# Fewer, longer f32 stretches between the projection's matmuls in a hybrid decoder layer

## What is computed

```python
u = rmsnorm(h, norm_w)
proj = jnp.einsum('btd,dc->btc', u, w_in)
...
dec_strict = jnp.exp(jnp.where(strict, diff, -jnp.inf))
A = beta[..., None] * jnp.einsum('bhtd,bhsd->bhts', k, k) * dec_strict
lhs = jnp.eye(C, dtype=A.dtype) + A
rhs = jnp.concatenate([beta[..., None] * v, (beta * jnp.exp(gam))[..., None] * k], axis=-1)
sol = lax.linalg.triangular_solve(lhs, rhs, left_side=True, lower=True)
```

## Time and profile before

| quantity | value |
|---|---|
| median of 3 runs | 692.07 us (691.67 to 693.25) |
| time of the profiled execution | 692.72 us, of which span 690.9 us |
| PE, matmuls | 673.3 us busy (97%), 4,585 instructions |
| PE, weight loads | 640.8 us busy |
| DVE | 413.5 us busy (60%) |
| ACT | 324.2 us busy (47%) |
| POOL | 375.8 us busy (54%) |
| mean granted TensorE clock | 0.995 of full speed |

### The profile page before, as it was taken

The page is one execution under the profiler, slowest core; times in us unless marked ns, Lnnn a source line. Parts: engine busy times, 40 slices in busy tenths (PEclk is TensorE's granted clock), DMA queues, the critical chain, the costliest instruction groups (busy, mean ns, idle before and its releaser), DMA issues. The chain is left out here.

```text
span 690.9 us, 13130 instructions
## 1 busy us (share of the span) xinstructions
PE 673.3 (97%) x4585; PEld 640.8 (93%) x4585; DVE 413.5 (60%) x977; ACT 324.2 (47%) x918; POOL 375.8 (54%) x581
## 2 busy tenths in 40 slices
PE   6999999999999999999999999999999999999995
PEld 4799999989999999999999999999999998888884
DVE  7836446278882472597933634888426257866256
ACT  7545432746654416466445254555452354242333
POOL 4547342268773343587824343887442559866324
PEclk9999999999999999999999999999999999999998
DMA  8744334221214347532548332023254325212014
GB/s 277 72 45 83 31 35 84 27 32 32 42 34 62 51 74 37 24 24 37 39 57 72 70 43 31 2 39 51 55 85 145 90 64 189 85 55 84 1 61 183
DMA packets 64004, 44.96 MB, mean 65 GB/s; under 512 B 17446, under 2 KB 59044, under 8 KB 63940
## 3 DMA queue, kind: packets, MB, share of 16 engines
q1 hardware_dynamic: 63764, 43.81, 36.0%
q10 hardware_dynamic: 176, 0.33, 0.1%
HBM read 35.88 MB, written 7.65 MB: 63 GB/s over the span
## 5 line engine op out<-in xcount | busy, mean ns | idle before, releaser
L283 PE MATMUL proj<-uTh,w_high 128*128 128x352 f32 (+4 forms) x768 | 262.0, 341 | 0.0
L283 PE MATMUL proj<-uTh,w_low 128*128 128x352 f32 (+4 forms) x768 | 245.7, 320 | 0.0
L283 PE MATMUL proj<-uTl,w_high 128*128 128x352 f32 (+4 forms) x768 | 245.2, 319 | 0.0
L283 PEld LDWEIGHTS proj<-uTh,w_high 128*128 128x128 f32 x768 | 145.1, 189 | 0.2
L283 PEld LDWEIGHTS proj<-uTl,w_high 128*128 128x128 f32 x768 | 145.1, 189 | 0.0
L283 PEld LDWEIGHTS proj<-uTh,w_low 128*128 128x128 f32 x768 | 144.3, 188 | 0.0
L326 POOL TENSOR_TENSOR w_low<-w_raw,w_high 128x256 fp32r<-128x256 f32 (+1 forms) x54 | 76.1, 1420 | 47.2 <-DVE decay L379 26.8
L1356 POOL TENSOR_TENSOR level_k<-hg_k,f_suffix 128x64 f32<-128x64 f32 (+1 forms) x144 | 64.4, 467 | 10.5 <-PE mix L1827 5.0
L1366 POOL TENSOR_TENSOR f_suffix<-f_suffix,f_prefix 128x192 f32<-128x192 f32 x84 | 52.3, 622 | 17.8 <-DVE f_prefix L1621 6.0
L1668 DVE SCALAR_TENSOR_TENSOR conv_out<-conv_in,hg_taps,conv_out 128x352 f32<-128x352 f32 (+2 forms) x81 | 55.2, 681 | 0.0
L1621 DVE TENSOR_TENSOR f_prefix<-f_prefix 128x192 f32<-128x192 f32 x84 | 43.9, 523 | 13.9 <-POOL f_suffix L1366 13.1
(11 more groups left out here) (331 smaller groups left out, 1416.3 us busy)
## 6 DMA issues: line engine op xcount, KB each, us to landing
w_raw<-in_w_in SPq DMA_DIRECT2D x32, 512.0 KB, 8.5
x_tile<-in_x SPq DMA_DIRECT2D x8, 512.0 KB, 8.5
w_raw<-y_scratch SPq DMA_DIRECT2D x8, 384.0 KB, 4.4
decay<-gamma_scratch SPq DMA_DIRECT2D x4, 576.0 KB, 3.7
landing<-in_w_out SPq DMA_DIRECT2D x4, 512.0 KB, 7.8
landing<-in_x SPq DMA_DIRECT2D x3, 512.0 KB, 8.3
out_y<-landing SPq DMA_DIRECT2D x3, 512.0 KB, 2.6
y_scratch<-gd_y SPq DMA_DIRECT2D x6, 192.0 KB, 2.6
```

The costliest lines, as they stand in the source:

```text
L283: last = pe.matmul(acc[:, 0:tw], w[j % 2][:, k, :], u[:, k, t0:t0 + tw], start=(k == 0 and i == 0), stop=(k == KT - 1 and i == 2))
```

## The change

The number of projection parts behind the f32 blocks is dealt out anew. Among the groups, three blocks get none behind them, so that A1 of group 0 runs into A1 of 1, A3 of 0 into A1 of 2, and A3 of 1 into A2 of 2: nine stretches of f32 work become six, with the same 32 parts between them. The parts over the small inverses go from 38 to 42. In the levels, parts stand only behind Z4 and Z5 (5 each, `("mixed", i)`): Y4 runs into Z4, TN4 into Y5 and Z5, TN5 into Y6 and Z6, so eight stretches become three. The end of the phase gets 9 parts in place of 4. The order of the f32 blocks, every matmul and every piece stay the same.

On ACT, the three decay exponentials, which stood one in each level, move ahead to the time of the small inverses, before the second half of the parts there. A one-element Silu behind them (`primer`) has ACT load the Silu table at once.

```diff
+        primer = sb("silu_primer", [P, 1], F32, st)
...
-            give((s, g), (4, 4, 4, 4, 4, 3, 3, 3, 3)[n])
+            give((s, g), (0, 7, 5, 0, 7, 5, 0, 5, 3)[n])
         give(("blocks", 0), 10)
-        give(("blocks", 1), 28)
+        give(("blocks", 1), 16)
+        give(("blocks", 2), 16)
         for i in MIXED:
...
-            give(("B1", i), 3)
-            give(("B2", i), 2)
             if i < LEVELS - 1:
-                give(("B3", i), 2)
+                give(("mixed", i), 5)
...
             take_hg(act, parts[("blocks", 1)])
+            if more:
+                for g in range(NG):
+                    decay_exp(act, g, dec_sub, dec_exp)
+                act.activation(primer[:, :], cc[:, 0, 0:1], ACT.Silu)
+            take_hg(act, parts[("blocks", 2)])
...
                 if more:
-                    decay_exp(act, i - BASE, dec_sub, dec_exp)
                     if i == BASE:
                         split_high(act, 4)
...
-                take_hg(act, parts[("B1", i)])
-                take_hg(act, parts[("B2", i)])
                 if i < LEVELS - 1:
+                    take_hg(act, parts[("mixed", i)])
...
-                project(pe, parts[("B1", i)])
...
-                project(pe, parts[("B2", i)])
                 if i < LEVELS - 1:
+                    project(pe, parts[("mixed", i)])
...
-                    project(pe, parts[("B3", i)])
             project(pe, parts[("end",)])
```

More of the change, by code:

```diff
@@ L2124, in _ @@
                         wo_highs(act, (4,))
-                    take_hg(act, parts[("B3", i)])
             take_hg(act, parts[("end",)])
@@ L2297, in _ @@
             project(pe, parts[("blocks", 1)])
+            project(pe, parts[("blocks", 2)])
             for i in MIXED:
```

## The result

The changed kernel takes 694.58 us (median of five runs, 694.19 to 695.05); the kernel before takes 691.86 us beside it (five runs, 691.47 to 693.25). The ratio is 1.0036, with a 95% interval of 1.0024 to 1.0047: slower by 0.4%, some 2.5 us. (The ratios in this document are worked out from the single runs of both kernels; they are not the quotients of the medians.) The forecast was 694.0 us.

A forecast was written before the change was run, and what follows sets the result against it. PE alone was taken to bound the delta phases. Waits for ACT's copies, 0.41 to 0.56 us a phase, taken as 1.9 us over four phases, added to the 692.07 us median gave 694.0 us; range 691.2 to 696.5 us.

The forecast's parts named there:

- Joining saves nothing: Joined blocks among the groups and joined Y and Z: 0.00 us saved each, bounds 0 and 0.08.
- Rival 2: Each change between projection and f32 work costs 0.08 us: 689.4 us without waits (12%), 691.3 us with them (5%).
- Level 4 to 5: Behind TN4, Y5's first matmul waits for ACT's copy of group 0: 0.15 us lost a phase.
- the allowance: Up to 0.05 us extra at each of three waiting places, for one more step in PE's queue; an estimate.
- Level 5 to 6: Behind TN5, Y6 waits for ACT's copy, shorter transposes hiding less: 0.23 us lost a phase.
- Y to Z: Z waits for ACT's copy of Y, tightest at group 2 of level 6: 0 to 0.03 us lost.
- The sum: Waits in the levels: 0.41 us a phase, 0.56 with allowances; four phases 1.6 to 2.2 us, taken as 1.9.
- The groups: Group blocks keep their places to within one part and nothing new is awaited there; no cost counted.
- The moved exponentials: ACT's chain ahead of the second hg_v copy is hidden before the fourth weight tile: price 0, cover 1.5 us.
- rival 3: ACT's chain ends over 1.5 us later than forecast, PE waits at the fourth weight tile: 697.3 us, chance 7%.
- The fewer table loads are worth nothing.: Two ACT table loads a phase in place of four gain nothing, since ACT's time was not on PE's path.
- The drain behind a table load: The skill's extra 1.38 us per table switch does not show; by that rule PE loses some 1.2 us in three phases.

The follow-up runs named there:

- the exponentials alone: Kernel before with only the three decay exponentials and the one-element Silu moved ahead, f32 blocks where they were: 692.49 us against 692.20, ratio 1.0004.
- more hand-overs: Kernel before with 60 more changes between projection and f32 work, same matmuls: 693.21 us against 692.82, ratio 0.9998.
- the groups alone: Kernel before with only the parts among the group blocks dealt out anew: 692.87 us against 692.82, ratio 1.0003.
- one part behind each TN, old groups: Changed kernel with one of five parts put behind TN4 and TN5, and the groups' parts dealt as before: 692.16 us against 692.20, ratio 0.9996.
- one part behind each TN: Changed kernel with one of the five parts ahead of TN4 and of TN5 put behind it: 693.47 us against 692.82, ratio 1.0008.
- one part behind TN5: Changed kernel with one part put behind TN5 only, TN4 still running into Y5: 693.49 us against 692.20, ratio 1.0017.
- the levels alone: Kernel before with only the levels joined as in the change, groups and exponentials where they were: 697.16 us against 692.82, ratio 1.0056.
- two more table loads: Changed kernel with a one-element exponential and another one-element Silu behind the primer: 696.98 us against 692.20, ratio 1.0071.

## Why the prediction was right, point by point

The time, 694.58 us, is 0.6 us above the forecast, 0.1 us past the likeliest case's own range (693.3 to 694.5) and inside the range given. The sign, the places and the mechanism were right. One term of 0.3 us was missing, two small terms were mis-sized in opposite directions, and one cover was larger than read. In the traces, the sum of terms can be checked more closely. What each kernel's phases take more than those of before, divided by the time before, lies inside the interval of its measured ratio every time:

| kernel | delta phases, us more than before | over 692 us | measured ratio |
|---|---|---|---|
| the exponentials alone | 0.05 | 1.0001 | 1.0004 [0.9994, 1.0014] |
| more hand-overs | 0.11 | 1.0002 | 0.9998 [0.9984, 1.0012] |
| the groups alone | 0.93 | 1.0013 | 1.0003 [0.999, 1.0015] |
| one part behind each TN, old groups | 0.17 | 1.0002 | 0.9996 [0.9987, 1.0005] |
| one part behind each TN | 0.38 | 1.0005 | 1.0008 [0.9996, 1.0021] |
| one part behind TN5 | 1.26 | 1.0018 | 1.0017 [1.0008, 1.0025] |
| after | 2.34 | 1.0034 | 1.0036 [1.0024, 1.0047] |
| the levels alone | 4.32 | 1.0062 | 1.0056 [1.0036, 1.0075] |
| two more table loads | 4.90 | 1.0071 | 1.0071 [1.0057, 1.0085] |

- **What bounds the kernel.** Right. Apart from the stops named above, PE fills the phase in every trace, and 2.4 us less of ACT's time in a phase is worth nothing by itself (the exponentials alone).
- **Joining saves nothing.** Right for the groups' blocks, shown from both sides: 12 transposes in one block cost twice 6, and 60 more hand-overs cost nothing. Rival 2, a price of 0.08 us, is out, and the 0.40 us record behind such a block is no time of PE's. The joined Y and Z were priced at 0.00 with a bound of 0.08; they saved 0.02 to 0.05 us each, 0.10 us a phase. The prediction looked for such a remainder at A1, Y4 and TN4 and found one at TN4 only; it did not take the distance across a Z block.
- **Level 4 to 5.** Right in place and mechanism: forecast 0.15 us, up to 0.20 with the allowance, and 0.22 measured. The hand-over from ACT to PE was read as 0.16 us from a wait elsewhere; 0.15 stands in the row after. The rest, 0.07 us, is the longer step from the first to the second instruction of Y5, which the sum had only as an allowance of 0.05.
- **Level 5 to 6.** Forecast 0.23 us, up to 0.28 with the allowance, and 0.27 measured, again with 0.08 us more than usual from the first to the second instruction of Y6.
- **Y to Z.** The place was right, group 2 of level 6. The size was forecast as 0 to 0.03 us, up to 0.08 with the allowance, and 0.09 is measured. In the sum it does not show, because the joined Y and Z give back 0.10.
- **The sum.** Forecast 0.41 to 0.56 a phase and 1.9 us in all; the parts behind TN take away 1.93 us. That the two agree so well is partly luck. The waits of Y5 and Y6 were forecast at 0.38 us without allowances and cost 0.49, and the two terms that cancel, 0.09 and 0.10, were in the sum as 0.03 and 0.
- **The groups.** "The blocks of the groups keep their places to within one part" and nothing new is awaited there: true, but the term of zero was 0.3 us short, the stretch in the table above. No wait is recorded there. The distances between projection matmuls of 352 columns are 159.7 ns on the mean in each phase of before, one of 39 being 165 ns or more; in after they are 160.8 in the first phase and 161.7 or 161.8 in the others, where eight or nine of 41 are 165 ns or more. That is why the delta phases grew by 2.34 and not by 1.9.
- **The moved exponentials.** Their price of 0 is right, and rival 3 needs ACT to be later than it is. The cover was mis-sized: forecast 1.5 us, 2.4 by the rows after and 2.1 by the two extra loads. The three exponentials overlap, 1.36 us for 3 x 0.53, and the first load does not wait for DVE's differences.
- **"The fewer table loads are worth nothing."** Against the kernel before, yes. But the sentence took ACT's queue in the levels as it was before, and in the joined order the load ahead of the hg_z copy would stand in front of TN4's copies. The levels alone show it: joined without the move, they lose 4.3 us, more than the whole change. I counted the copies as free "in the new order too", which was right, and missed that it is so only because the load is gone. (That run puts back the exponential and both its loads together. By an estimate from its rows the second load, 1.28 us, is enough to make the copies late: without it they could begin at 271.30 - 1.28 = 270.02, ahead of the 270.52 at which they begin when nothing holds them up.)
- **The drain behind a table load.** In the trace of after the ACTIVATE behind a table load starts 1.29 us behind the start of the load, and in the one with two more loads a further load starts 0.01 us behind the small ACTIVATE. The Trainium skill (ScalarE: Activation LUTs, What ACT_TABLE_LOAD costs) adds about 1.38 us of drain to each switch. Neither trace agrees: with it, two switches would have held the chain up by 3.0 + 2 x 1.38 = 5.8 us, and PE by 5.8 - 2.1 = 3.7 us in place of 0.86, an estimate from the figure of that section.

**What stays open.** The 0.04 to 0.10 us a phase among the groups: why in some phases eight or nine of the distances between projection matmuls are 165 ns or more and in others one is. It was not tried to hold ACT, DVE and POOL still during that stretch. Also open is why joining Y and Z saves 0.02 to 0.05 us; the rows show where, not why. The measured difference, 2.5 us by the ratio and 2.7 by the medians, is 0.2 to 0.4 us more than the 2.34; that is inside the uncertainty of the ratio (0.24% to 0.47%, 1.7 to 3.3 us).

## What to carry to other kernels

Where an engine is the bound and works through two kinds of work, first ask what a change between them costs, by dividing the distance across a short and across a long block by their instructions; if both give the same, longer stretches gain nothing. Do it for each kind of block: here the blocks with the shortest instructions had a remainder and the others none. Filler between a producer and its consumer is there for the other engine's copy: before taking it away, add up copy and hand-over, and leave just as much as they need (0.47 us was enough here). An edit that is worth nothing by itself can be what keeps a second edit cheap, so try both alone before one of them is called idle.

## What was not expected of the hardware

A stop of PE of 0.2 to 0.3 us leaves no entry in its list of waits when transposes or matmuls stand in front of it, since their records are longer (0.83 us for eight transposes that take 0.70) than their own time; distances between starts show it, and so does the list of its weight loads (0.17 and 0.23 us). Behind such a stop the second instruction follows the first 0.07 to 0.08 us later than it does without one. A switch of ACT's table costs the load alone, 1.28 us and 0.01 to 0.02 us around it. The same 39 distances between projection matmuls on PE have a mean of 159.8 ns in one phase and 161.3 in the next (the levels alone, second and third phase), with the same instructions on PE.
